# Attention of differences: three row blocks' scores move into the values' projection, and the order of the row blocks changes

## The chip, the cores and the metric

The kernel runs on one core of a Trainium2 chip. The metric is the time of one execution on the device, in microseconds (us), and the figure compared is the median of several executions.

## What is computed

Four layers in a row on a sequence of 1024 rows and 1024 features, in f32. The first two (a dilated attention and a latent attention) and the large MLPs are untouched. The change lies in the mixer of the third and of the fourth layer, which are alike. In them the core of the reference is:

```python
proj = h @ w_in[l]
q_da, k_da, v_da, q_r, k_r, v_r, g_r, u_pool = jnp.split(proj, split_points, axis=-1)
...
lam = (jnp.exp(jnp.sum(lq1.astype(jnp.float32) * lk1.astype(jnp.float32)))
       - jnp.exp(jnp.sum(lq2.astype(jnp.float32) * lk2.astype(jnp.float32))) + lam_init)
...
    s = jnp.einsum('bhmqd,bhmkd->bhmqk', q_blk, k).astype(jnp.float32) * scale
...
```

Each of four heads has two maps (m) of 64 features. Both maps get a causal softmax over the keys, and the output of the head is (softmax of map 0 minus lam times softmax of map 1) times the values of 128 features, normalised per row. Beside it the mixer has a retention of four heads, and a mean over windows of 2, 4, 8 and 16 rows ("pool"). The three outputs are joined and projected by w_out.

## The kernel before

Every engine has its own program, and the order of work is written out by hand in each: the PE program issues matmuls in the order of the code, and waits stand where an instruction needs another engine's result. All matmuls are recorded by one helper, so that a row of the profile says L130 and is told apart by its tiles.

**Projection.** `pe_mix` makes the parts of `h @ w_in` in the order `PARTS = [3, 0, 1, 4, 5, 2]`; part 2, the last, is the values v_da (tile c_v). `pe_tiles` makes a part of eight row tiles in two groups of four (g or b is 0 and 1), each over eight weight blocks k. A weight block is loaded by SP into one of eleven slots (`NS = 11`, tile wst), and split by POOL into whi and wlo; a product takes three matmuls (thi*whi, thi*wlo, tlo*whi). The four tiles of either group of part 2 lie in PSUM banks 0 to 3 (ring "proj"), and ACT copies them to c_v.

**Attention.** The work is cut into 32 units of one head h and one block j of 128 query rows; a unit of block j sees j + 1 blocks of keys, so its width w is 128 * (j + 1). `UNITS` gives the order: in each head j goes 7, 6, ... 0. The PE loop of `pe_diff` does in its iteration i:

- the scores of unit i: for both maps, a matmul of c_q with c_k per 512 keys (64 rows of the array, ps<-c_k,c_q), then a small bf16 matmul that adds the causal mask (ps<-cst_cmask,cst_idb). Map 0 has banks 0 and 1, map 1 banks 2 and 3 (ring "s2"), whatever the width, and the scores of a unit wait until ACT has read those of the unit before,
- a turn of the window output (`WINDOWS`, ps<-s_wa,r_pw) or of the retention's (`RET_TURNS`, ps<-cst_ident,c_rn) in some iterations,
- the transposes of unit i-3's probabilities (ps<-cst_ident,tfl or r_p) into banks 4 and 5,
- the product of unit i-4's transposed probabilities with the values (ps<-c_v,tfl or tfi) into bank 6 or 7.

DVE does per iteration: the maxima of both maps (TENSOR_REDUCE cst_sm<-ps), the low half of a window or retention output (tlo<-ps,thi), which needs ACT's high half, then the mixing of the two maps of unit i-1 (SCALAR_TENSOR_TENSOR tfl<-p_p,cst_sm,tfl), then the copy of the second half of unit i-3's transposes. ACT does: the two exponentials of unit i (tfl, r_p or p_p<-ps,cst_sm), a high half (thi<-ps), the copy of the first four transposed blocks of unit i-3, and the scaling and the squares of unit i-4's output. So the chain through a unit is: scores, maximum of map 0, exponential of map 0, scores of the next unit.

Of the kernel before, what the change touches and what calls it, by code (L numbers as in the profile page):

```python
# [16 lines left out]
NS = 11  # L17
# [156 lines left out]
class Banks:  # L174
# [4 lines left out]
             "s3": [(0,), (1,)], "t3": [(2,), (3,)], "d3": [(4,), (5,)], "o3": [(6,)], "a3": [(7,)], "t2": [(4,), (5,)], "o2": [(6,), (7,)],  # L179
# [94 lines left out]
class Kernel:  # L274
# [355 lines left out]
    def pe_tiles(self, pe, st, nk, items, nb, ring, terms, wkey, ready, kready=None, after=None, amid=None):  # L630
# [4 lines left out]
        for g, size in enumerate(sizes):  # L635
# [3 lines left out]
            for it in group:  # L639
                B.take((st, it), ring)  # L640
# [1534 lines left out]
    def pe_mix(self, q, l):  # L2175
# [8 lines left out]
        for n in self.PARTS:  # L2184
            def amid(b, k):
# [11 lines left out]
            self.pe_tiles(q, ("c", l, n), 8, items, (3, 3, 2) if n == 3 and l == 0 else 4, "proj", terms, lambda k: ("c", l, n, k),  # L2197
# [7 lines left out]
    def act_mix(self, q, l):  # L2205
# [151 lines left out]
    def sp_borrow(self, sp, l):  # L2357
# [39 lines left out]
    def pe_diff(self, q, l):  # L2397
        S, B, ps = self.S, self.B, self.ps
        q.wait_ge(*S.at("mask"))
        for i in range(32 + 4):  # L2400
            if i < 32:
                h, j = self.UNITS[i]
                w = 128 * (j + 1)
                bs = [B.take(("cs", l, i, mp), "s2") for mp in range(2)]
                q.wait_ge(*B.done(("ct", l, "q", 7)))
                q.wait_ge(*B.done(("ct", l, "k", 7)))
                for c in range(0, w, 512):
                    n = min(512, w - c)
                    for mp in range(2):
                        if c == 0:  # L2410
                            for event in B.freed(("cs", l, i, mp)):
                                q.wait_ge(*event)
                        r = slice(64 * mp, 64 * mp + 64)
                        q.matmul(ps[:, bs[mp] + c // 512, 0:n], self.cq[r, h, blk(j)], self.ck[r, h, c:c + n], start=True,
                                 stop=(c + n < w), skip_group_check=True)
                for mp in range(2):
                    q.matmul(ps[:, bs[mp] + c // 512, n - 128:n], self.idb[:], self.cmask[:], start=False, stop=True,
                             skip_group_check=True).then_inc(*S.up("qk", ("c", l, i, mp)))
            if i in self.WINDOWS and self.WINDOWS[i][1] is not None:
# [34 lines left out]
    def act_diff(self, q, l):  # L2454
        S, B, ps = self.S, self.B, self.ps
        for i in range(32 + 4):
            if i < 32:
                h, j = self.UNITS[i]
                w = 128 * (j + 1)
                for mp in range(2):  # L2460
                    key = ("cs", l, i, mp)
                    b = B.of(key)
                    q.wait_ge(*S.at("c_max", (l, i, mp)))
                    if mp == 0:
                        if i >= 4:
                            q.wait_ge(*S.at("turned", ("cT", l, i - 4, self.UNITS[i - 4][1] // 4)))
                    elif i >= 2:
                        q.wait_ge(*S.at("c_mix", (l, i - 2)))
                    dst = self.p1[i % 4] if mp == 0 else self.p2[i % 2]
                    q.activation(dst[:, 0:w], ps[:, b:b + 2, :].rearrange("p a b -> p (a b)")[:, 0:w], ACT.Exp,  # L2470
                                 bias=self.cstat(i, 2 + mp), accum_out=self.cstat(i, 4 + mp)).then_inc(*B.free(key, "exp"))
            if i in self.WINDOWS and self.WINDOWS[i][1] is not None:
# [39 lines left out]

    def act_diff_hi(self, q, l, h):
# [7 lines left out]
    def dve_diff(self, q, l):  # L2521
        S, B, ps = self.S, self.B, self.ps
        q.wait_ge(*S.at("tile", (("c", l, 2), 7)))
        q.memset(self.pw[:], 0.0).then_inc(*S.up("pw_zero", l))
        q.memset(self.wa[:, 0:16], 0.0)
        q.memset(self.wb[:, 0:16], 0.0).then_inc(*S.up("mix_zero", l))
# [791 lines left out]
```

## Time and profile before

| | us |
|---|---|
| median of 3 runs | 4079.43 (4076.68 to 4085.45) |
| the profiled execution, its own time | 4081.01 |
| its span in the trace | 4079.2 |
| PE busy | 3882.3 |
| DVE busy | 2207.4 |
| ACT busy | 1436.9 |
| POOL busy | 1906.9 |
| attention of the third layer, scores of unit 0 to the first matmul of the output projection | 1899.46 to 2060.22 |
| the same of the fourth layer | 3113.24 to 3275.48 |

The two attention stages are 160.8 and 162.2 us of the span. A busy PE is not a PE at its peak: the matmuls' ends are modelled, and at the lower clock the same matmul is counted longer. The granted clock (PEclk) is 1.00 for 2.4 GHz and 0.50 for 1.2 GHz.

### The profile page before, as it was taken

Reading aid. Unit: us, or ns where it says so; the run is one execution under the profiler, and the core shown is the slowest. Engines: PE = TensorE matmul, PEld = TensorE weight load, DVE = VectorE, ACT = ScalarE, POOL = GpSimd, SP = SyncE. Lnnn points to the kernel's source line nnn. Section 1 sums busy time; section 2 is a strip of 40 time slices with the busy share of each in tenths; the row PEclk is TensorE's granted clock in tenths of the full one; section 3 lists DMA queues with packets and bytes.
Section 4 is the critical chain, followed back from the end, with each engine's and each line's share of the span. In section 5 each row is a group of like instructions: output and inputs, shape, how many; then the busy total and the mean of one; then the engine's idle time right before and its main releaser. Section 6 shows DMA issues by size and latency. Waiting matters only on the chain.

```text
span 4079.2 us, 49896 instructions
## 1 busy us (share of the span) xinstructions
PE 3882.3 (95%) x19191; PEld 3140.4 (77%) x19191; DVE 2207.4 (54%) x3488; ACT 1436.9 (35%) x2928; POOL 1906.9 (47%) x1707
## 2 busy tenths in 40 slices
PE   8999999999999999999898999999998898999998
PEld 4677788777888887786576788888786577788887
DVE  2242426482777775632637777624633638777633
ACT  1122223133666662222634333312222634333211
POOL 1313122272333334522234788986522135778975
PEclk9999999999999999999899999999998899999999
DMA  5312221232000003110022222453210033222543
GB/s 178 115 51 79 67 64 42 86 103 62 6 10 7 11 6 110 64 33 17 1 97 96 83 80 86 149 170 123 96 36 8 1 107 97 77 88 78 172 158 129
DMA packets 247508, 310.37 MB, mean 76 GB/s; under 512 B 38804, under 2 KB 161060, under 8 KB 247272
## 3 DMA queue, kind: packets, MB, share of 16 engines
q1 hardware_dynamic: 214456, 231.87, 18.5%
q10 hardware_dynamic: 32816, 75.32, 5.3%
q8 instruction: 152, 2.49, 0.2%
q14 instruction: 84, 0.69, 0.1%
HBM read 253.48 MB, written 51.53 MB: 75 GB/s over the span
## 4 chain that ended last, share of the span: by engine, by line
PE 73%; DVE 16%; ACT 4%; issue 4%; POOL 2%; DMA 1%; ACTq 0%; SPq 0%; DVEq 0%; POOLq 0%
PE ps L130 69%; PE ps L133 4%; DVE cst_sm L153 3%; DVE ml_p L142 3%; ACT thi L136 2%; DVE da_sg L159 1%; POOL wlo L142 1%; DVE tlo L142 1%; DVE f_ta L150 1%; DVE f_tb L150 1%; ACT ml_o L136 1%; ACT tfi L136 0%; POOL whi L139 0%; DVE tfl L142 0%; POOL mlo_z L142 0%
## 5 line engine op out<-in xcount | busy, mean ns | idle before, releaser
L139 POOL CAST whi<-wst 128x512 fp32r<-128x512 f32 (+3 forms) x524 | 424.5, 810 | 1429.8 <-DMA wst<-in_a_w_in 457.7
L142 POOL TENSOR_TENSOR wlo<-wst,whi 128x512 fp32r<-128x512 f32 (+2 forms) x650 | 926.8, 1433 | 42.1
L130 PE MATMUL ps<-whi,thi 128*128 128x512 f32 (+3 forms) x1816 | 707.5, 390 | 19.8 <-POOL wlo L142 6.0
L130 PE MATMUL ps<-whi,tlo 128*128 128x512 f32 (+3 forms) x1816 | 685.2, 377 | 0.0
L130 PE MATMUL ps<-wlo,thi 128*128 128x512 f32 (+3 forms) x1816 | 684.2, 377 | 0.0
L130 PEld LDWEIGHTS ps<-whi,thi 128*128 128x128 f32 x1816 | 344.5, 190 | 102.6 <-issue 25.6
L130 PEld LDWEIGHTS ps<-wlo,thi 128*128 128x128 f32 x1816 | 344.7, 190 | 58.1 <-issue 3.8
L130 PEld LDWEIGHTS ps<-whi,tlo 128*128 128x128 f32 x1816 | 343.7, 189 | 57.5
L130 PE MATMUL ps<-thi,whi 128*128 128x512 f32 x856 | 339.4, 397 | 15.7 <-POOL wlo L142 10.9
L130 PE MATMUL ps<-tlo,whi 128*128 128x512 f32 x856 | 337.8, 395 | 0.0
L130 PE MATMUL ps<-thi,wlo 128*128 128x512 f32 x856 | 337.3, 394 | 0.0
L153 DVE TENSOR_REDUCE cst_sm<-ps 128x1 f32<-128x1024 f32 (+7 forms) x256 | 246.5, 984 | 75.5 <-PE ps L130 75.5
L130 PEld LDWEIGHTS ps<-thi,whi 128*128 128x128 f32 x856 | 163.4, 191 | 53.1 <-POOL wlo L142 13.6
L130 PE MATMUL ps<-mla_kh,thi 128*128 128x512 f32 x512 | 192.0, 416 | 1.9 <-ACT tfi L136 1.9
L150 DVE SCALAR_TENSOR_TENSOR f_tb<-f_ub,tfi,f_tb 128x1024 f32<-128x1024 f32 x88 | 190.7, 2167 | 1.6
L130 PEld LDWEIGHTS ps<-thi,wlo 128*128 128x128 f32 x856 | 163.5, 191 | 34.7
L130 PEld LDWEIGHTS ps<-tlo,whi 128*128 128x128 f32 x856 | 163.5, 191 | 33.8
L136 ACT ACTIVATE thi<-ps 128x512 fp32r<-128x512 f32 (+2 forms) x258 | 141.1, 565 | 137.4 <-PE ps L133 132.8
L136 ACT ACTIVATE whi<-wst 128x512 fp32r<-128x512 f32 x126 | 70.5, 620 | 279.1 <-DVE wst L142 241.3
L130 PE MATMUL ps<-c_k,c_q 64*128 64x512 f32 (+3 forms) x384 | 131.8, 631 | 36.4 <-ACT tfl L136 35.1
L142 POOL TENSOR_TENSOR tlo<-tfl,thi 128x512 fp32r<-128x512 f32 x96 | 152.8, 1597 | 6.1 <-ACT thi L136 1.1
L145 POOL TENSOR_SCALAR tfl<-tfl,cst_sm 128x64 f32<-128x64 f32 x128 | 56.7, 443 | 182.5 <-DVE cst_sm L159 176.2
(389 smaller groups left out, 8244.6 us busy)
## 6 DMA issues: line engine op xcount, KB each, us to landing
wst<-in_w_down SPq DMA_DIRECT2D x140, 256.0 KB, 3.2
wst<-in_w_up SPq DMA_DIRECT2D x126, 256.0 KB, 3.0
scr_h<-f_tb SPq DMA_DIRECT2D x44, 512.0 KB, 4.0
wst<-in_w_in SPq DMA_DIRECT2D x64, 256.0 KB, 2.7
wst<-in_a_w_in SPq DMA_DIRECT2D x72, 192.0 KB, 2.4
wst<-in_ada_w SPq DMA_DIRECT2D x48, 256.0 KB, 3.4
da_am<-in_ada_w SPq DMA_DIRECT2D x48, 256.0 KB, 2.7
f_T2lw<-scr_h SPq DMA_DIRECT2D x48, 256.0 KB, 3.8
```

Source lines behind the costliest of these rows:

```text
L130: return self.none if self.e is None else self.e.matmul(*a, **k)
L133: return self.none if self.e is None else self.e.transpose(*a)
L136: return self.none if self.e is None else self.e.activation(*a, **k)
L139: return self.none if self.e is None else self.e.tensor_copy(*a)
L142: return self.none if self.e is None else self.e.tensor_tensor(*a)
L145: return self.none if self.e is None else self.e.tensor_scalar(*a)
L150: return self.e.scalar_tensor_tensor(out=out, in0=a, scalar=s, in1=b, op0=o1, op1=o2, **k)
L153: return self.none if self.e is None else self.e.tensor_reduce(*a, **k)
L159: return self.none if self.e is None else self.e.reciprocal(*a)
```

## The change

- Units 0, 1 and 2 are scored inside the second group of part 2, before its weight blocks k = 2, 4 and 6 (`FIRST_UNITS`). The second group's four tiles take banks 4 to 7 (ring "tr4"), so that banks 0 to 3 are there for the scores. ACT does the three units' exponentials before it copies the second group's tiles, and DVE's loop starts with them; its clearing of r_pw, s_wa and s_wb stands behind unit 3's maxima.
- The order of a head is j = 7, 5, 0, 4, 6, 3, 1, 2.
- A unit with j below 4 needs one bank for each map and takes it from the ring "s1", banks 0, 2, 1, 3 in turn.
- The window outputs are turned at iterations 8, 9, 15 and 16 instead of 5, 6, 11 and 12.
- The weights of part 2 start in slot 9, so that the planes and slots which units 0 to 2 write are free by then. In the third layer six slots are passed over (3 to 8); in the fourth the part began in slot 9 already. SP's instructions stay the same in number and order.

```diff
@@ class Banks @@
-             "s3": [(0,), (1,)], "t3": [(2,), (3,)], "d3": [(4,), (5,)], "o3": [(6,)], "a3": [(7,)], "t2": [(4,), (5,)], "o2": [(6,), (7,)],
+             "s1": [(0,), (2,), (1,), (3,)], "s3": [(0,), (1,)], "t3": [(2,), (3,)], "d3": [(4,), (5,)], "o3": [(6,)], "a3": [(7,)], "t2": [(4,), (5,)], "o2": [(6,), (7,)],
@@ def pe_tiles @@
-                B.take((st, it), ring)
+                B.take((st, it), ring if isinstance(ring, str) else ring[g])
@@ def sp_mix @@
+            while n == 2 and self.wn % NS != 9:
+                self.wn += 1
@@ def pe_mix, amid(b, k) @@
+                if n == 2 and b and k in self.FIRST_UNITS:
+                    self.pe_scores(q, l, self.FIRST_UNITS[k])
...
+                          ("proj", "tr4") if n == 2 else "proj", terms, lambda k: ("c", l, n, k),
@@ def act_mix @@
+                if n == 2 and b:
+                    for i in range(3):
+                        self.act_exp(q, l, i)
@@ units @@
-    UNITS = [(h, j) for h in range(4) for j in range(7, -1, -1)]
+    UNITS = [(h, j) for h in range(4) for j in (7, 5, 0, 4, 6, 3, 1, 2)]
-    WINDOWS = {1: (0, None), 5: (0, 0), 6: (0, 1), 7: (1, None), 11: (1, 0), 12: (1, 1)}
+    WINDOWS = {8: (0, 0), 9: (0, 1), 15: (1, 0), 16: (1, 1)}
+    FIRST_UNITS = {2: 0, 4: 1, 6: 2}
@@ def pe_diff, act_diff @@
-        for i in range(32 + 4):
+        for i in range(3, 32 + 4):
@@ def pe_scores @@
+        bs = [B.take(("cs", l, i, mp), "s1" if j < 4 else "s2") for mp in range(2)]
@@ def act_exp @@
+            if mp == 0:
+                if i >= 4:
+                    q.wait_ge(*S.at("turned", ("cT", l, i - 4, self.UNITS[i - 4][1] // 4)))
+                else:
+                    q.wait_ge(*S.at("tile", ("w", ("c", l, 2, i))))
+            elif i >= 2:
+                q.wait_ge(*S.at("c_mix", (l, i - 2)))
```

On PE, at the end of the values' projection of the third layer (matmuls with whi, wlo, thi and tlo are the projection) and the start of the attention, the program before reads:

```order
 L130 MATMUL ps<-wlo,thi 128x512
 L130 MATMUL ps<-whi,tlo 128x512
 L130 MATMUL ps<-c_k,c_q 128x512 x4
 L130 MATMUL ps<-cst_cmask,cst_idb 128x128 x2
 L130 MATMUL ps<-c_k,c_q 128x512 x2
 L130 MATMUL ps<-c_k,c_q 128x384 x2
 L130 MATMUL ps<-cst_cmask,cst_idb 128x128 x2
 L130 MATMUL ps<-c_k,c_q 128x512 x2
```

and the program of the change reads, in the middle of the projection, at unit 1:

```order
 L130 MATMUL ps<-wlo,thi 128x512
 L130 MATMUL ps<-whi,tlo 128x512
 L130 MATMUL ps<-c_k,c_q 128x512 x2
 L130 MATMUL ps<-c_k,c_q 128x256 x2
 L130 MATMUL ps<-cst_cmask,cst_idb 128x128 x2
 L130 MATMUL ps<-whi,thi 128x512
 L130 MATMUL ps<-wlo,thi 128x512
 L130 MATMUL ps<-whi,tlo 128x512
```

Before, nothing but a wait stands between the scores of the first three units; now 24 matmuls of the projection do, and at its end the first transposes (of unit 0) follow the scores of unit 3.

On PE in the second head, from the scores of unit 10 on (c_k,c_q are scores, cst_ident transposes, c_v the product with the values), the program of before is:

```order
 L130 MATMUL ps<-c_k,c_q 128x384 x2
 L130 MATMUL ps<-cst_cmask,cst_idb 128x128 x2
 L133 MATMUL ps<-cst_ident,tfl 128x128 x6
 L130 MATMUL ps<-c_v,tfi 128x128 x7
 L130 MATMUL ps<-c_k,c_q 128x256 x2
 L130 MATMUL ps<-cst_cmask,cst_idb 128x128 x2
 L133 MATMUL ps<-cst_ident,r_p_167 128x128 x5
 L130 MATMUL ps<-c_v,tfl 128x128 x6
```

and that of the change:

```order
 L130 MATMUL ps<-c_k,c_q 128x128 x2
 L130 MATMUL ps<-cst_cmask,cst_idb 128x128 x2
 L133 MATMUL ps<-cst_ident,r_p_167 128x128 x3
 L130 MATMUL ps<-c_v,tfl 128x128 x2
 L130 MATMUL ps<-c_k,c_q 128x512 x2
 L130 MATMUL ps<-c_k,c_q 128x128 x2
 L130 MATMUL ps<-cst_cmask,cst_idb 128x128 x2
 L133 MATMUL ps<-cst_ident,tfl 128x128 x8
```

The first of the two pieces is from units 13 and 14 of before (j = 2 and 1), the second from units 10 and 11 of the change (j = 0 and 4): long runs of transposes and value products stood behind narrow scores, and now narrow scores have few of them behind them and a wide unit has eight transposes.

## Rows read from the trace of the kernel before

**Rows 1.** The page: the chain that ended last, by engine.
```profile
PE 73%; DVE 16%; ACT 4%; issue 4%; POOL 2%; DMA 1%; ACTq 0%; SPq 0%; DVEq 0%; POOLq 0%
```
**Rows 2.** Stretches of both layers: length, busy time and instructions, granted clock.
```profile
core 0: us, PE busy (x) PEld busy (x) DVE busy (x) ACT busy (x) POOL busy (x), PEclk, DMA share, GB/s
1855.68:1899.46 43.78, 43.69 (x193) 35.89 (x192) 3.13 (x9) 6.57 (x12) 0.00 (x0) 1.00 0.00 1
1899.46:1917.99 18.53, 11.85 (x31) 5.11 (x31) 9.31 (x15) 7.30 (x13) 9.20 (x6) 0.65 0.06 12
1917.99:2051.42 133.43, 116.66 (x635) 77.90 (x635) 91.68 (x167) 79.55 (x234) 26.68 (x24) 0.86 0.00 1
2051.42:2060.22 8.80, 7.61 (x66) 6.91 (x65) 3.78 (x14) 7.66 (x30) 1.98 (x3) 1.00 0.42 130
...
3113.24:3131.30 18.06, 11.38 (x30) 4.56 (x30) 9.79 (x15) 7.29 (x13) 9.19 (x6) 0.69 0.06 12
3131.30:3266.39 135.09, 117.06 (x635) 77.75 (x635) 92.22 (x167) 79.59 (x234) 26.66 (x24) 0.85 0.00 1
3266.39:3275.48 9.09, 7.87 (x65) 6.92 (x65) 3.78 (x14) 7.95 (x30) 2.53 (x4) 1.00 0.46 129
```
**Rows 3.** Waits within 1899 to 2060: total us, times, longest.
```profile
ACT tfl L136 <- DVE cst_sm L153: 48.1, 24, 4.8
...
DVE cst_sm L153 <- PE ps L130: 35.4, 21, 4.9
```
**Rows 4.** Timeline of PE, third head: start, us, instruction, count, idle before.
```profile
1978.27 1.99 PE L130 MATMUL ps<-c_k,c_q 64*128 64x512 f32 x8
...
1982.97 2.90 PE L130 MATMUL ps<-c_k,c_q 64*128 64x512 f32 x8 [1.27 <-ACT tfl L136]
...
1988.35 2.96 PE L130 MATMUL ps<-c_k,c_q 64*128 64x512 f32 x8 [1.37 <-ACT tfl L136]
...
2002.35 1.95 PE L130 MATMUL ps<-c_v,tfl 128*128 128x128 f32 x16
2004.23 0.92 PE L130 MATMUL ps<-c_k,c_q 64*128 64x384 f32 x4
...
2011.69 0.49 PE L130 MATMUL ps<-c_k,c_q 64*128 64x128 f32 x4
...
2014.13 0.99 PE L130 MATMUL ps<-c_k,c_q 64*128 64x512 f32 x2
```
**Rows 5.** Timelines of DVE and ACT, the softmax of a unit with j = 7.
```profile
1980.46 2.36 DVE L153 TENSOR_REDUCE cst_sm<-ps 128x1 f32<-128x1024 f32 x2 [2.36 <-PE ps L130]
...
1981.71 1.11 ACT L136 ACTIVATE tfl<-ps,cst_sm 128x1024 f32<-128x1024 f32 x1 [2.54 <-DVE cst_sm L153]
...
1983.86 0.19 ACT L136 ACTIVATION_READ_ACCUMULATOR p_p<-ps,cst_sm 128x1 f32 x1
```
**Rows 6.** Timeline of DVE, unit 21, an iteration with a retention output.
```profile
2006.04 1.01 DVE L153 TENSOR_REDUCE cst_sm<-ps 128x1 f32<-128x384 f32 x2
2008.17 0.42 DVE L142 TENSOR_TENSOR tlo<-ps,thi 128x256 fp32r<-128x256 f32 x1 [1.11 <-ACT thi L136]
...
2009.96 0.74 DVE L153 TENSOR_REDUCE cst_sm<-ps 128x1 f32<-128x256 f32 x2
```
**Rows 7.** Timeline of PE, units 25 and 26, at a clock of 0.50 from 2023.
```profile
2019.13 3.72 PE L130 MATMUL ps<-c_k,c_q 64*128 64x512 f32 x8 [1.27 <-ACT tfl L136]
...
2025.38 3.92 PE L130 MATMUL ps<-c_k,c_q 64*128 64x512 f32 x8 [0.50 <-ACT tfl L136]
...
2031.60 1.22 PE L130 MATMUL ps<-c_k,c_q 64*128 64x512 f32 x1 [0.90 <-ACT tfl L136]
```
**Rows 8.** Timelines of DVE and POOL: mixing 384 keys twice, and POOL's windows.
```profile
1938.12 2.33 DVE L150 SCALAR_TENSOR_TENSOR tfl<-p_p,cst_sm,tfl 128x384 f32<-128x384 f32 x1
...
2052.25 0.62 DVE L150 SCALAR_TENSOR_TENSOR tfl<-p_p,cst_sm,tfl 128x384 f32<-128x384 f32 x1
...
1938.14 1.89 POOL L142 TENSOR_TENSOR s_wa<-s_wb 128x1024 f32<-128x1024 f32 x1
```
**Rows 9.** The page's loads of w_in, and POOL's split of a weight block.
```profile
wst<-in_w_in SPq DMA_DIRECT2D x64, 256.0 KB, 2.7
...
1850.43 0.61 POOL L139 CAST whi<-wst 128x512 fp32r<-128x512 f32 x1 [0.84 <-DMA wst<-in_w_in]
1851.12 1.29 POOL L142 TENSOR_TENSOR wlo<-wst,whi 128x512 fp32r<-128x512 f32 x1
```

More of the change, by code:

```diff
@@ L2398, in pe_diff @@
         S, B, ps = self.S, self.B, self.ps
-        q.wait_ge(*S.at("mask"))
-        for i in range(32 + 4):
+        for i in range(3, 32 + 4):
             if i < 32:
[L2402 to L2419, printed above, removed]
+                self.pe_scores(q, l, i)
+            if i in self.WINDOWS:
                 self.pe_window(q, l, *self.WINDOWS[i])
@@ L2444, in pe_diff, with pe_scores @@
             self.pe_diff_turn(q, l, h, "tr4")
+    FIRST_UNITS = {2: 0, 4: 1, 6: 2}
+    def pe_scores(self, q, l, i):
+        S, B, ps = self.S, self.B, self.ps
+        q.wait_ge(*S.at("mask"))
+        h, j = self.UNITS[i]
+        w = 128 * (j + 1)
+        bs = [B.take(("cs", l, i, mp), "s1" if j < 4 else "s2") for mp in range(2)]
+        q.wait_ge(*B.done(("ct", l, "q", 7)))
+        q.wait_ge(*B.done(("ct", l, "k", 7)))
+        for c in range(0, w, 512):
+            n = min(512, w - c)
+            for mp in range(2):
+                if c == 0:
+                    for event in B.freed(("cs", l, i, mp)):
+                        q.wait_ge(*event)
+                r = slice(64 * mp, 64 * mp + 64)
+                q.matmul(ps[:, bs[mp] + c // 512, 0:n], self.cq[r, h, blk(j)], self.ck[r, h, c:c + n], start=True,
+                         stop=(c + n < w), skip_group_check=True)
+        for mp in range(2):
+            q.matmul(ps[:, bs[mp] + c // 512, n - 128:n], self.idb[:], self.cmask[:], start=False, stop=True,
+                     skip_group_check=True).then_inc(*S.up("qk", ("c", l, i, mp)))
     def pe_diff_turn(self, q, l, h, ring):
@@ L2449, in pe_diff_turn, with banks @@
                          [self.S.at("c_scaled", (l, h))])
+    def banks(self, b, w):
+        return self.ps[:, b, 0:w] if w <= 512 else self.ps[:, b:b + 2, :].rearrange("p a b -> p (a b)")[:, 0:w]
     def cstat(self, i, n, w=1):
@@ L2455, in act_diff @@
         S, B, ps = self.S, self.B, self.ps
-        for i in range(32 + 4):
+        for i in range(3, 32 + 4):
             if i < 32:
[L2458 to L2472, printed above, removed]
+                self.act_exp(q, l, i)
+            if i in self.WINDOWS:
                 m, hf = self.WINDOWS[i]
@@ L2511, in act_diff, with act_exp @@
             self.act_diff_hi(q, l, h)
+    def act_exp(self, q, l, i):
+        S, B, ps = self.S, self.B, self.ps
+        w = 128 * (self.UNITS[i][1] + 1)
+        for mp in range(2):
+            key = ("cs", l, i, mp)
+            b = B.of(key)
+            q.wait_ge(*S.at("c_max", (l, i, mp)))
+            if mp == 0:
[5 more added lines that the diff above has]
+                q.wait_ge(*S.at("c_mix", (l, i - 2)))
+            dst = self.p1[i % 4] if mp == 0 else self.p2[i % 2]
+            q.activation(dst[:, 0:w], self.banks(b, w), ACT.Exp,
+                         bias=self.cstat(i, 2 + mp), accum_out=self.cstat(i, 4 + mp)).then_inc(*B.free(key, "exp"))
     def act_diff_hi(self, q, l, h):
@@ L2522, in dve_diff @@
         S, B, ps = self.S, self.B, self.ps
[L2523 to L2526, printed above, removed]
         for i in range(32 + 4):
@@ L2534, in dve_diff @@
                     q.wait_ge(*S.at("qk", ("c", l, i, mp)))
-                    q.tensor_reduce(self.cstat(i, 2 + mp), ps[:, b:b + 2, :].rearrange("p a b -> p (a b)")[:, 0:w], AXX,
+                    q.tensor_reduce(self.cstat(i, 2 + mp), self.banks(b, w), AXX,
                                     ALU.max, negate=True).then_inc(*S.up("c_max", (l, i, mp)))
-            if i == 2:
+            if i == 3:
+                q.wait_ge(*S.at("tile", (("c", l, 2), 7)))
+                q.memset(self.pw[:], 0.0).then_inc(*S.up("pw_zero", l))
+                q.memset(self.wa[:, 0:16], 0.0)
+                q.memset(self.wb[:, 0:16], 0.0).then_inc(*S.up("mix_zero", l))
+            if i == 7:
                 q.wait_ge(*S.at("ld_mix", l))
@@ L2540, in dve_diff @@
                     *S.up("v_seq", ("sgm", l)))
-            if i in self.WINDOWS and self.WINDOWS[i][1] is not None:
+            if i in self.WINDOWS:
                 m, hf = self.WINDOWS[i]
```

4 lines of the change are left out of this document (2 added, 2 removed).

## The prediction

> **What bounds the kernel now.** The page's chain [rows 1] says that PE carries 73% of what ended last, DVE 16%. That is an average over all stages, so the next view is the two stages that the change touches, cut at their joints [rows 2]. In the values' projection (1855.68 to 1899.46) PE is busy all the time at clock 1.00 while DVE works 3.1 and ACT 6.6 of 43.8 us: PE alone bounds it. From 1899.46 to 1917.99, units 0 to 2, PE is busy only 11.9 of 18.5 us, and that at clock 0.65: nothing but three softmaxes one after another, since scores wait for the exponentials of the unit before. The fourth layer has the same, 18.06. From unit 3 to unit 31's scores it takes 133.4 and 135.1 us, with DVE busy 92 and ACT 80: no engine is full. The waits [rows 3] say how it turns: ACT waits 48 us for DVE's maxima, DVE 35 us for PE's scores, and PE in turn waits for ACT at the wide units, 1.27 and 1.37 us in [rows 4]. A loop of latencies bounds the wide units, PE's own work the narrow ones.
>
> **Part 1: three units inside the projection.** Removed: 18.5 and 18.1 us before unit 3's scores, mean 18.3. Added to the projection: PE's work for the three units. With its banks free a unit of j = 7 takes from 1978.27 to the maxima at 1980.46 [rows 4, 5], 2.2 us; one of j = 0 takes 0.5 and the mask's 0.2 [rows 4], 0.7; j = 5 lies between, 1.8. Sum 4.7. The step from projection to scores shows a start at 1899.46 where the matmul before it began at 1898.98 and the usual spacing is 43.78 / 192 = 0.23, so some 0.25 is lost at such a step; there are six, of which I count 1.0 in all. Part 1 costs 5.7 and gives 12.6 per layer. The bounds of the six steps are 0 and 6 x 0.5 = 3.0.
> The Trainium skill (TensorEngine Tiling (Array Packing), Key Properties) says that a change of the tiling mode drains the engine, which speaks against 64-row matmuls between 128-row ones. By that rule with 0.5 a step the part would give 10.6 instead of 12.6.
> Its cover: after unit 0's scores PE has two weight blocks, 2 x 43.78 / 16 = 5.5 us, before unit 1's. The softmax of unit 0 takes from the maxima at 1980.46 to the last exponential at 1984.05 [rows 5], 3.6 us, and unit 1's first scores need only map 0's. Margin 1.9 us. If that cover were gone, PE would stop for up to 3.6 us a unit in the projection. ACT copies the first group before that, and the second group's tiles behind unit 2's exponentials, which fall before the group's end; unit 0's transposes wait for that copy, some 1 us behind unit 3's scores, which hide it.
> Moved: in the third layer the weights of part 2 skip six slots. Its first block then waits until PE is through with block 3 of part 5 (eight blocks at 2.74 us that end at 1855.68), four blocks before that end, at 1844.7; it lands 2.7 later and is split in 1.9 [rows 9], at 1849.3, and PE wants it at 1855.7. Margin 6.4 us, the same for the following blocks, which come as fast as PE uses them. Cost nothing; with the cover gone it would be the excess over 6.4, once.
>
> **Part 2: the order.** I lay out one head at full clock, scores to scores, without window or retention outputs. Pieces: wide unit to wide unit 4.70 and 5.38 [rows 4], growing about 0.4 with each key block (maximum and exponential 0.14 each, scores 0.2); eight blocks of value product 1.95, so 0.24 a block [rows 4]; a transpose 0.12.
> Old order, 7 to 0: 4.7, 5.4, 4.8, 4.5 by the loop, then by PE (scores + transposes + product of wide units) 4.3, 3.6, 3.0, 2.5. Sum 32.8.
> New order: 7 to 5 4.7; 5 to 0 4.9; 0 to 4 2.9 (scores of map 1 wait for the second exponential of 5, and DVE mixes unit 7 first); 4 to 6 3.5; 6 to 3 5.5 by PE (2.9 + 6 transposes + 8 blocks); 3 to 1 3.3; 1 to 2 1.9 (own banks, no wait); 2 to 7 3.5 by PE. Sum 30.2.
> Retention outputs: there DVE's loop is maximum, both exponentials, ACT's high half, DVE's low half, mixing, copy; for unit 21 it is 3.92 us [rows 6]. Before, these eight iterations hold j = 3 to 0 and cost 1.2 a head over the plain ones. Now they hold 6, 3, 1, 2; by the same pieces unit 20 takes 5.5, and the delays add up to 3.9 at the next head. Windows: four iterations, 4.2 before, 3.9 now. Whole, from unit 3 to unit 31: before 19.9 + 35.0 + 34.0 + 31.3 = 120.2, now 17.8 + 33.4 + 34.8 + 29.0 = 115.0. The order gives 5.2. The traced 133.4 and 135.1 stand 13 to 15 above my sum, and I keep that rest but for two changes.
> First, the clock: at 0.86 over 133.4 us, 2 x 0.14 x 133.4 = 37 us ran at half. The cycle 25 to 26 takes 6.25 at half [rows 7] and its equal 17 to 18 5.38 [rows 4]: 16%, so 37 us hold 5.1 us of loss. The low stretches stand where wide units follow each other; now at most two do. I take half of it back, 2.6; bounds 0 and 5.1.
> Second, POOL: DVE's mixing of 384 keys takes 2.33 us beside POOL's windows and 0.62 without [rows 8]. Before, the first windows ran at units 0 and 1 with DVE idle; now they run at units 3 to 5, and three mixings meet them. DVE has 1 to 2 us of slack there; I charge 1.5, bounds 0 and 3 x 1.7 = 5.1.
> The Trainium skill (SBUF — State Buffer, Who interferes with whom) says that a VectorE instruction with two SBUF inputs contends with a GpSimd instruction that reads SBUF. By that rule the trace agrees, and the case in which it decides is the second rival below.
>
> **Part 3: the end.** From unit 31's scores to the output projection it takes 8.8 and 9.1 us [rows 2]. What is still to be transposed and multiplied then were units of j = 3, 2, 1, 0 (10 blocks; with the product of j = 4 15) and are now 6, 3, 1, 2 (16 and 21): six more of each, 6 x 0.36 = 2.2, and a longer last mixing. Loss 2.5. Weights of w_out are asked for at the same retention turn (unit 31) as before and have that much longer.
>
> Per layer: 12.6 + 5.2 + 2.6 - 1.5 - 2.5 = 16.4; two layers 32.8. From the execution of the trace, 4081.0, that is 4048.2; it stands 1.6 above the median shown, so the forecast for the median is **4047**.
>
> **Rivals.** (a) *The clock stays up.* If waits of PE are all short, the whole 5.1 comes back and half of what is left of the rest, (14 - 5.1) / 2 = 4.4, goes too: 16.4 + 2.5 + 4.4 = 23.3 per layer, 4033. For it: PE's work per head (36 blocks at 0.24 and 0.12, scores 0.5 + 0.21 a block, in all 24.6) fills 30.2 us better than 32.8. Against: PE's waits are 1.3 us at a time already in [rows 4], and the clock is 0.86 all the same.
> (b) *The order gives nothing.* Retention outputs beside a wide unit, and mixings beside POOL's, eat the 5.2, and no clock comes back: 12.6 - 1.5 - 2.5 = 8.6 per layer, 4062; with the upper bound on POOL 5.0, 4069. For it: DVE is then busy 92 of 128 us, in a loop that also holds ACT. Against: half of these iterations are narrow.
> (c) *The projection waits.* If unit 0's softmax is not done at block 4, PE stops there: 1.9 us margin, at most 3.6 for each of two units, so 9 per layer left, 4061. Speaks against it that DVE and ACT are idle there.
> (d) *Slower.* If the scores inside it brought the projection's second half down to clock 0.50, its 21.9 us would take as much again: 16.4 - 21.9 = -5.5 per layer, 4090. It decides from 16.4 us of PE time lost there on. In [rows 2] the clock is 1.00 wherever PE has no gaps and 0.65 where it waits a third of the time; the scores bring no wait of that size.
> (e) *Nothing moves*: softmax in the projection hidden but given back at the end, since the end waits for weights. They are asked for at unit 31 in any case, so hardly possible.
>
> **How the numbers follow.** Forecast (4040 to 4055) 0.45; (a) 0.23; (b) 0.20; (c) 0.06; (d) 0.04; (e) 0.02. The range goes from (a) with a little more to (b)'s worse bound: 4028 to 4067. A measurement tells 0.2%, 8 us, from no change. Faster by more than that, below 4071: all but (d) and (e), 0.94; same 0.03; slower 0.03.
>
> **What would show it.** Right: c_k,c_q matmuls three times inside the second half of the values' projection with PE idle before none of them for ACT, that half about 5.7 us longer at clock 1.00; unit 3's scores right behind it; 33 to 36 us from one unit of j = 7 to the next; a clock above 0.86; mixings of 1.5 to 2.5 us beside s_wa at units 3 to 5; 11 us from unit 31's scores to the output projection. Wrong: an idle PE in front of unit 1's or 2's scores, maxima that start long after their scores in iterations 8, 9, 16, 20 and 28, or a head above 36 us. The estimate stands weakest on the rest of 14 us that I carry over.

## The result and the profile after

The changed kernel takes 4046.63 us (median of 4 runs, 4041.24 to 4050.95) where the kernel before, in the same series, took 4078.05 (4075.16 to 4085.45): a ratio of 0.992, with a 95% interval of 0.9908 to 0.9932. The forecast was 4047. This section and the one on why the forecast was right show that the sum came out right while several of its terms did not.

The page of the changed kernel names the same engines in its chain as [rows 1]:

```profile
PE 72%; DVE 16%; ACT 4%; issue 4%; POOL 2%; DMA 1%; ACTq 0%; SPq 0%; DVEq 0%; POOLq 0%
```

The stages, cut as in [rows 2] (the first six rows are the third layer: the values' projection up to unit 3's scores, units 3 to 8, 8 to 16, 16 to 24, 24 to 31, and the end up to the output projection; the last three are the fourth layer's projection, units 3 to 31, and end):

```profile
core 0: us, PE busy (x) PEld busy (x) DVE busy (x) ACT busy (x) POOL busy (x), PEclk, DMA share, GB/s
1857.59:1905.97 48.38, 48.38 (x220) 37.53 (x218) 15.63 (x21) 12.79 (x24) 10.38 (x10) 1.00 0.07 23
1905.97:1925.44 19.47, 16.46 (x107) 10.90 (x107) 16.21 (x33) 11.86 (x36) 9.79 (x6) 1.00 0.08 12
1925.44:1962.03 36.59, 31.81 (x180) 21.68 (x179) 27.91 (x43) 21.85 (x67) 26.94 (x23) 0.91 0.00 0
1962.03:1997.58 35.55, 30.70 (x184) 21.48 (x183) 24.17 (x49) 23.01 (x71) 0.94 (x2) 0.95 0.01 1
1997.58:2031.86 34.28, 27.97 (x157) 19.85 (x156) 23.18 (x44) 21.68 (x60) 0.00 (x0) 0.87 0.00 1
2031.86:2044.30 12.44, 10.63 (x84) 9.12 (x83) 5.19 (x16) 9.69 (x34) 4.06 (x5) 0.95 0.38 113
3055.57:3103.94 48.37, 48.37 (x219) 37.53 (x217) 10.68 (x21) 12.78 (x24) 0.00 (x0) 1.00 0.00 1
3103.94:3230.22 126.28, 105.46 (x621) 72.97 (x620) 91.58 (x166) 78.33 (x228) 37.57 (x30) 0.93 0.01 3
3230.22:3244.53 14.31, 11.95 (x83) 10.40 (x83) 6.17 (x18) 10.30 (x34) 4.42 (x6) 0.88 0.43 134
```

PE is busy through the whole projection at clock 1.00, which is now 48.4 us instead of 43.8 in [rows 2]: 4.60 for three units, and nothing in front of unit 3. Units 3 to 31 take 125.9 and 126.3 us (before 133.4 and 135.1), the end 12.4 and 14.3 (before 8.8 and 9.1). From the start of the third layer's values' projection to its output projection it is 186.7 us, before 204.5 (1855.68 to 2060.22): 17.8 less. In the fourth it is 189.0 against 206.0, which is 17.0 less. The forecast had 16.4 each. The two stages give 34.9; the spans differ by 31.9. Over all the traces here, what lies between the stages differs by up to 2.4 us, what lies behind them by 3.0, and what lies ahead of them by 6.6 (the values' projection starts at 1852.1 to 1858.7).

The scores in the projection, on PE's timeline (start, us, instruction, count, idle before), with the projection's own matmuls left out:

```profile
1884.88 1.99 PE L130 MATMUL ps<-c_k,c_q 64*128 64x512 f32 x8
1886.80 0.28 PE L130 MATMUL ps<-cst_cmask,cst_idb 128*128 128x128 bf16 x2
...
1892.55 1.56 PE L130 MATMUL ps<-c_k,c_q 64*128 64x512 f32 x8
...
1899.80 0.49 PE L130 MATMUL ps<-c_k,c_q 64*128 64x128 f32 x4
1900.22 0.28 PE L130 MATMUL ps<-cst_cmask,cst_idb 128*128 128x128 bf16 x2
...
1905.97 1.24 PE L130 MATMUL ps<-c_k,c_q 64*128 64x512 f32 x6
```

No row has an idle time. The three units take 2.20, 1.78 and 0.71 us from first to last matmul, 4.69, and the projection grew by 4.60: beyond the scores' own extent the six steps between projection and scores cost nothing. Counted from start to start, as the forecast did, a step takes 0.32 us (the matmul before unit 0's scores starts at 1884.56, the scores at 1884.88) where the projection's spacing is 0.23: some 0.1 a step, which is then part of the 4.60. ACT is done with unit 0 at 1890.66:

```profile
1888.33 1.12 ACT L136 ACTIVATE tfl<-ps,cst_sm 128x1024 f32<-128x1024 f32 x1 [4.73 <-DVE cst_sm L153]
...
1890.47 0.19 ACT L136 ACTIVATION_READ_ACCUMULATOR p_p<-ps,cst_sm 128x1 f32 x1
```

That is 1.9 us before unit 1's scores at 1892.55, the margin of the forecast.

### The profile page after: what moved, and what is told of

Its sections match the earlier page's. It is cut to its first block, busy times and chain, and to the rows that moved or that the text cites. A ratio compares the mean times of both kernels' runs of the same rounds, so it can differ in the third digit from the quotient of the medians.

```text
span 4047.3 us, 49898 instructions
## 1 busy us (share of the span) xinstructions
PE 3858.2 (95%) x19191; PEld 3133.4 (77%) x19191; DVE 2216.1 (55%) x3488; ACT 1436.6 (35%) x2928; POOL 1912.2 (47%) x1707
## 4 chain that ended last, share of the span: by engine, by line
PE 72%; DVE 16%; ACT 4%; issue 4%; POOL 2%; DMA 1%; ACTq 0%; SPq 0%; DVEq 0%; POOLq 0%
PE ps L130 68%; PE ps L133 4%; DVE cst_sm L153 3%; DVE ml_p L142 3%; ACT thi L136 2%; DVE da_sg L159 1%; DVE tlo L142 1%; POOL wlo L142 1%; DVE f_ta L150 1%; DVE f_tb L150 1%; ACT ml_o L136 1%; ACT tfi L136 1%; POOL mix_z L142 0%; DVE tfl L142 0%; POOL whi L139 0%
## 5 line engine op out<-in xcount | busy, mean ns | idle before, releaser
L130 PE MATMUL ps<-whi,thi 128*128 128x512 f32 (+3 forms) x1816 | 709.2, 391 | 19.5 <-POOL wlo L142 7.4
L130 PE MATMUL ps<-thi,whi 128*128 128x512 f32 x856 | 339.6, 397 | 15.3 <-POOL wlo L142 11.7
L136 ACT ACTIVATE tfi<-ps,cst_sm 128x1024 f32<-128x1024 f32 (+1 forms) x160 | 130.7, 817 | 24.8 <-DVE cst_sm L153 20.1
## 6 DMA issues: line engine op xcount, KB each, us to landing
wst<-in_a_w_in SPq DMA_DIRECT2D x72, 192.0 KB, 2.5
```

The source lines that it names most:

```text
L130: return self.none if self.e is None else self.e.matmul(*a, **k)
L136: return self.none if self.e is None else self.e.activation(*a, **k)
```

## The experiments

All times are medians. The stage time is from the start of the values' projection to the output projection in the profiled execution, third and fourth layer.

| kernel | us | stages, us |
|---|---|---|
| before | 4078 to 4080 | 204.5, 206.0 |
| the change | 4046.63, again 4044.08 | 186.7, 189.0; again 188.5, 187.6 |
| placement alone (with the new window places) | 4040.63 | 186.7, 187.5 |
| order, ring and window places alone | 4063.40 | 197.2, 197.4 |
| window places alone | 4063.48 | 197.8, 198.2 |
| narrow units on two banks a map | 4045.94 | 188.2, 188.8 |
| no window sums, in the change | 4031.16 | 182.0, 182.0 |
| no window sums, before | 4071.04 | 203.3, 201.8 |
| new order in heads 1 and 2 only | 4036.32 | 184.7, 184.6 |
| the same, windows later | 4044.45 | 187.6, 186.5 |
| placement alone, windows later | 4055.69 | 194.7, 192.8 |
| unit 0 a block later | 4048.00 | 188.5, 192.0 |
| window sums in halves | 4040.59 | 185.2, 187.5 |

### The parts of the change

**Placement alone.** The order is put back, all units are on "s2".

```diff
-    UNITS = [(h, j) for h in range(4) for j in (7, 5, 0, 4, 6, 3, 1, 2)]
+    UNITS = [(h, j) for h in range(4) for j in range(7, -1, -1)]
-        bs = [B.take(("cs", l, i, mp), "s1" if j < 4 else "s2") for mp in range(2)]
+        bs = [B.take(("cs", l, i, mp), "s2") for mp in range(2)]
```

> The change with the order of the row blocks put back to 7, 6, ... 0 and all units on two banks a map; units 0 to 2 stay in the projection, the windows at iterations 8, 9, 15, 16. My theory (the placement carries most): the three units removed 18.3 us and the projection grew by 4.6 in the trace of the change, so 13.7 per layer, less up to 1.5 for POOL's windows beside the mixings, and the end stays at 9: 24 to 27 us in all, 4051 to 4054. Rival 1 (the order carries half): 4060 or more. Rival 2 (the order gives nothing in sum, its longer end eats it): 4047, as the change.

4040.63 us, ratio to before 0.9911 (0.9896 to 0.9925). What the second rival says of the order is true, it gives nothing in sum, and the placement (here with the new window places) is worth more than any of the cases had. Its stages (third layer, the six cuts as above):

```profile
1854.65:1904.33 49.68, 49.68 (x224) 37.91 (x222) 17.36 (x21) 14.08 (x24) 10.36 (x10) 1.00 0.07 22
1904.33:1922.00 17.67, 15.50 (x119) 11.72 (x118) 14.83 (x33) 11.25 (x36) 10.65 (x6) 1.00 0.07 14
1922.00:1959.90 37.90, 31.99 (x180) 20.58 (x180) 28.67 (x45) 23.12 (x68) 27.96 (x24) 0.91 0.00 0
1959.90:1995.75 35.85, 32.68 (x184) 21.75 (x183) 23.61 (x49) 21.80 (x66) 0.08 (x1) 0.86 0.01 1
1995.75:2032.54 36.79, 31.19 (x161) 20.65 (x160) 23.77 (x44) 23.25 (x66) 0.00 (x0) 0.86 0.00 1
2032.54:2041.32 8.78, 7.61 (x66) 6.90 (x65) 3.77 (x14) 7.63 (x29) 1.96 (x3) 1.00 0.42 123
```

Against these the new order gains 1.3 us in the projection (its three units are narrower), loses 1.8 in units 3 to 8, gains 1.3, 0.3 and 2.5 in the three heads behind, and loses 3.7 at the end: together 0.05 us worse, and in the fourth layer 1.4. The change run again gives 1.8 and 0.1 us worse.

**Order alone.** Units 0 to 2 go back behind the projection (`FIRST_UNITS = {}`, the loops of PE and ACT from 0, no exponentials in `act_mix`).

> The change with units 0 to 2 taken out of the projection again; order, rings and window places of the change. Theory: unit 3 to unit 31 gains 7.5 and 8.8 us by the trace of the change, the end loses 3.6 and 5.2, so 3.8 per layer; in front the units 7, 5, 0 need some 2 us less than 7, 6, 5. Together 8 to 12 us: 4066 to 4070. Rival (order and placement only help together): within 3 us of before, 4075 to 4078. Rival (the order carries more than the placement): below 4060.

4063.40 us, 0.996 (0.9947 to 0.9973). Better than I expected, and placement (39 us below before) plus this (16) is far more than both together (31 to 35): the two kernels share a part. They share the new places of the windows; they also share the second group's banks 4 to 7, DVE's later clearing and the weights' slots, so the next run takes the windows' places by themselves.

**Window places alone.** One line of the kernel before:

```diff
-    WINDOWS = {1: (0, None), 5: (0, 0), 6: (0, 1), 7: (1, None), 11: (1, 0), 12: (1, 1)}
+    WINDOWS = {8: (0, 0), 9: (0, 1), 15: (1, 0), 16: (1, 1)}
```

> The kernel before with one edit: the window outputs are turned at iterations 8, 9, 15, 16 instead of 5, 6, 11, 12. The question is why units 3 to 8 took 23.4 us before and 17.7 with the placement alone. Theory A (the windows' places): the two turns leave iterations 5 and 6 and POOL's second set of sums no longer starts at iteration 7, where DVE's operations took 1.44 to 2.33 us instead of 0.22 to 0.62; 3 to 4 us less there, 1 us more in the second head: 2 to 3 per layer, 4072 to 4075. Theory B (the granted clock at the entry, 0.50 before and 1.00 behind the projection, explains all 5.7): 4077 to 4080 here.

4063.48 us, 0.9965 (0.9952 to 0.9977): theory A, but more than twice its size. The stages of this kernel (units 3 to 8, 8 to 16, 16 to 24, 24 to 31), and under them the same of before:

```profile
1919.12:1937.40 18.28, 17.81 (x116) 13.23 (x116) 13.26 (x31) 11.56 (x36) 0.00 (x0) 0.88 0.01 1
1937.40:1975.32 37.92, 31.99 (x179) 20.81 (x178) 28.66 (x44) 23.19 (x68) 27.97 (x24) 0.91 0.00 0
1975.32:2009.75 34.43, 30.68 (x184) 20.33 (x183) 23.63 (x49) 21.86 (x66) 0.07 (x1) 0.95 0.01 1
2009.75:2045.85 36.10, 30.21 (x159) 20.34 (x158) 23.77 (x44) 23.31 (x66) 0.00 (x0) 0.86 0.00 1
```

```profile
1917.99:1941.40 23.41, 19.82 (x121) 13.93 (x121) 17.05 (x32) 11.97 (x36) 6.96 (x4) 0.91 0.00 1
1941.40:1978.27 36.87, 32.00 (x177) 20.44 (x177) 28.78 (x48) 22.96 (x69) 19.72 (x21) 0.91 0.00 0
1978.27:2014.14 35.87, 31.77 (x182) 21.48 (x181) 22.08 (x44) 21.34 (x66) 0.00 (x0) 0.86 0.01 1
2014.14:2051.42 37.28, 33.06 (x160) 22.06 (x159) 23.77 (x44) 23.27 (x66) 0.00 (x0) 0.77 0.00 1
```

Units 3 to 8 take 18.3 instead of 23.4 us, the second head 1.0 more, the last two 1.4 and 1.2 less at a higher clock. Together 6.7 us in the third layer and 7.8 in the fourth. Of the 5.1 in the first stretch, 0.9 each is from the turns out of iterations 5 and 6 (cycles 4.20 and 3.65, now 3.29 and 2.75), and 3.3 from the cycle of unit 7 to 8 (5.52, now 2.20). There DVE stood beside POOL's second sums; the timeline of DVE in the kernel before:

```profile
1936.64 1.44 DVE L150 SCALAR_TENSOR_TENSOR cst_sm<-cst_sm,cst_lam 128x1 f32<-128x1 f32 x1
...
1941.15 1.52 DVE L150 SCALAR_TENSOR_TENSOR cst_sm<-cst_sm,cst_lam 128x1 f32<-128x1 f32 x1
```

An operation on one column, 0.22 us elsewhere, takes 1.4 to 1.5, twice around one narrow unit, with the 2.33 of [rows 8] between them. How much of the 3.3 is the sums' can be read from a run further down, the kernel before without the sums: there this cycle takes 3.08 us, so 2.4 are the sums' and 0.9 are not. On PE it is one wait, in the kernel before and, under it, without the sums:

```profile
1940.70 0.49 PE L130 MATMUL ps<-c_v,tfi 128*128 128x128 f32 x2 [2.79 <-DVE tfi L139]
```

```profile
1935.02 0.49 PE L130 MATMUL ps<-c_v,tfi 128*128 128x128 f32 x2 [0.34 <-DVE tfi L139]
```

So the three parts, each as the difference of two kernels, in the third and the fourth layer: window places 6.7 and 7.8 (before to window places), placement 11.2 and 10.6 (window places to placement alone; the second group's banks and the slots move with it), order with ring 0.0 and -1.4 (placement alone to the change).

**The ring.** `"s1" if j < 4 else "s2"` becomes `"s2"`.

> The change with the one-bank ring taken out: narrow units take two banks a map again, so the scores of j = 3, 1 and 2 wait for the exponentials of the unit before. My sum had 1.9 us from j = 1 to j = 2 with banks of their own where about 3 us would be needed without. Theory: 1 to 2 us a head, 8 to 14 us in all: 4055 to 4061. Rival (PE's transposes and products stand between them anyway, the banks are free in time): within 2 us of the change, 4045 to 4049.

4045.94 us, 0.9922 (0.9907 to 0.9937): the theory falls. The cycle of j = 1 to 2 does grow (1.63 to 2.83 us in the second head), but the one behind it shrinks (4.61 to 4.31), and units 24 to 31 take 34.9 instead of 34.3. In the stages it is 1.3 us in all, too little for the medians to tell.

**The heads apart.**

```diff
+    UNITS = [(h, j) for h in range(4) for j in ((7, 5, 0, 4, 6, 3, 1, 2) if h in (1, 2) else range(7, -1, -1))]
```

> The change with the new order in the second and third head alone; the first and the last head go 7, 6, ... 0. Theory (what the order gives is set head by head, by the stretches of the two traces): against the placement alone the new order gave 1.3 us in the second head and 0.3 to 1.5 in the third; in the last it gave 2.5 and cost 3.7 to 5.2 at the end, in the first it cost 0.5. So this kernel is 1.6 to 2.8 per layer better than the placement alone, 5 us better than the change or more: 4035 to 4038. Rival (the heads can't be taken apart, since the clock makes up the difference): 4040 to 4046.

4036.32 us, 0.9897 (0.9884 to 0.9911), the lowest median of a kernel that keeps the whole computation. Its interval overlaps that of the placement alone, so the medians don't part the two; the stages, 184.7 and 184.6 us, are 2.0 and 3.0 below the placement alone, and the end is back at 9.5 and 9.1. In these traces the new order pays in the middle heads, where its wide last units don't stand at the stage's end.

**The cover.** Unit 0 is scored before k = 3, so that one weight block is left between units 0 and 1.

```diff
-    FIRST_UNITS = {2: 0, 4: 1, 6: 2}
+    FIRST_UNITS = {3: 0, 4: 1, 6: 2}
```

> The change with unit 0 scored one weight block later, before k = 3, so that only one block (2.74 us) lies between units 0 and 1. I had counted a softmax of 3.6 us that the cover must hide. Theory: PE waits 0.8 to 0.9 us in front of unit 1 in each layer, nothing else moves: 1.7 us, 4048 with the change at 4046.6, and the waiting place is seen in the trace. Rival (the wait also lowers the granted clock in the projection): 5 us a layer and more, 4056. Rival (map 0's bank is free after 2.4 us already, so no wait): 4046.6.

4048.00 us, 0.9923 (0.991 to 0.9937). The projection is 49.24 us instead of 48.38 in both layers: 0.86, as the theory has it. (The fourth layer's 192.0 in the table holds a cycle of 7.9 us from unit 7 to 8; the change without this edit has it at 4.6 and 7.7 in one trace and at 6.2 and 4.8 in the other.) PE and ACT at that place:

```profile
1891.37 2.44 PE L130 MATMUL ps<-c_k,c_q 64*128 64x512 f32 x8
```

```profile
1890.99 1.11 ACT L136 ACTIVATE p_p<-ps,cst_sm 128x1024 f32<-128x1024 f32 x1
1892.00 0.19 ACT L136 ACTIVATION_READ_ACCUMULATOR p_p<-ps,cst_sm 128x1 f32 x1
```

The wait is not in front of unit 1 but inside it: map 0's scores find their banks free, map 1's wait for the exponential that ends at 1892.1, so that the eight matmuls take 2.44 us instead of 1.56. A timeline row that gathers matmuls can hide such a wait in its length.

### POOL's sums and DVE

**Without the sums.** In `pool_windows` one subtraction is left of each window; once in the change, once in the kernel before.

```diff
-            op(q.tensor_tensor(wa[:, 16:1040], u[:, 16:1040], u[:, 15:1039], ALU.add))
...
-            q.tensor_tensor(pl, pl, u[:, 16:1040], ALU.subtract).then_inc(*S.up("windows", (l, m)))
+            q.tensor_tensor(pl, u[:, 16:1040], u[:, 15:1039], ALU.subtract).then_inc(*S.up("windows", (l, m)))
```

> The change with POOL's sums over windows left out: one subtraction is left of each of the two windows' 6 to 8 operations, so the pool output is not the reference's. Theory: the clash of POOL's windows with DVE's mixings costs the 1.5 us per layer that I charged, up to 3 where unit 10's maxima were late: 3 to 6 us in all, 4041 to 4044. Rival (it lies in DVE's slack): 4046 to 4047.5.

> The kernel before with POOL's sums over windows left out (one subtraction is left of each), so the pool output is not the reference's. In the change the same edit gave 15.5 us. Theory (the change brought a new clash, since the first sums ran beside idle DVE before): here only the second sums cost, 3 to 4 us a layer: 4071 to 4073. Rival (the clash cost as much before, my charge of 1.5 for the difference holds): 12 to 15 us, 4063 to 4066.

4031.16 us in the change (0.9886, 0.9869 to 0.9902) and 4071.04 in the kernel before (0.9978, 0.9969 to 0.9987). In the stages the change loses 4.7 and 7.0 us with the sums gone, the kernel before 1.2 and 4.3: the sums cost the change 3.1 us per layer more on average. By the medians they cost 15.5 us in the change (12.9 against its second series) and 9.4 in the kernel before, so 1.7 to 3.0 more per layer. The stages hold 11.7 of the 15.5; for the rest the traces name no cause. DVE's busy time between units 3 and 31 falls from 91.5 to 83.4 us in the change:

```profile
1903.05:2022.65 119.60, 102.77 (x622) 71.65 (x621) 83.39 (x166) 78.00 (x228) 16.79 (x18) 0.94 0.02 3
```

Where it strikes in the change, fourth layer, DVE and POOL, and PE behind them:

```profile
3116.76 3.34 DVE L150 SCALAR_TENSOR_TENSOR tfl<-p_p,cst_sm,tfl 128x896 f32<-128x896 f32 x1
3120.02 0.74 DVE L153 TENSOR_REDUCE cst_sm<-ps 128x1 f32<-128x256 f32 x2
```

```profile
3116.79 2.36 POOL L142 TENSOR_TENSOR s_wa<-s_wa,c_pu 128x1024 f32<-128x1024 f32 x1
```

```profile
3118.78 0.28 PE L130 MATMUL ps<-cst_cmask,cst_idb 128*128 128x128 bf16 x2
3122.03 1.75 PE L133 MATMUL ps<-cst_ident,tfl 128*128 128x128 f32 x7 [2.97 <-ACT tfi L136]
```

A mixing of 896 keys takes 3.34 us instead of 1.15, the maxima of unit 6 start after it, 3.1 us behind their scores, and the cycle from unit 7 to 8 is 7.7 us, where it is 3.7 without the sums.

**Windows later.** To find what decides the price, the windows were turned at 11, 12, 18, 19, once with the mixed heads and once with the placement alone. The change ran again beside them.

> The changed kernel itself, in one series with the two below, so that they stand beside it and not beside a figure of another series. Expected 4045 to 4048; its two stages 186.7 and 189.0 us from the start of the values' projection to the output projection, with the fourth layer's cycle from unit 7 to 8 either 4.6 or 7.7.

> The kernel with the new order in the second and third head alone, and the window outputs at iterations 11, 12, 18, 19 instead of 8, 9, 15, 16. So POOL's second sums, which started behind iteration 9 and stood beside units 10 and 11 (cycle 6.5 instead of 5.3), start behind iteration 12. Theory (a sum costs where it stands beside a wide mixing): 1 to 2 us less at units 10 and 11, and up to as much again at the wide unit 16: 0 to 4 us in all, 4033 to 4036. Rival (it costs the same anywhere): 4036 to 4037, and rival (the two outputs of iterations 18 and 19 push the retention's): 4039 or more.

> The placement alone, order 7, 6, ... 0, with the window outputs at iterations 11, 12, 18, 19. Here the second sums stood beside units 10 and 11 (cycle 7.7 instead of 5.3) and would stand beside j = 3 to 0 and unit 16. Theory: the cycle from 10 to 11 comes back to 4.8 to 5.3, 2.4 less a layer, the turns in narrow iterations cost 0.9 each as they did at 5 and 6, and 1 us more at unit 16: 0 to 3 us in all, 4038 to 4041. Rival: the turns and sums beside narrow units stop PE as in the kernel before (7 to 8 took 5.5 instead of 2.2): 4045 or more.

4044.08 us (0.9912, 0.9896 to 0.9927), 4044.45 (0.9918, 0.9904 to 0.9931) and 4055.69 (0.9943, 0.9929 to 0.9957). Both late kernels are slower than their partners, by 8 and 15 us (by 4.9 and 13.3 in the two stages), so my theory that a sum costs where it stands beside a wide mixing falls. In the kernel with the placement alone the cycle of unit 13 to 14 (1953.34 to 1961.29) went from 3.3 to 8.0 us. DVE and POOL there and in the two cycles behind it:

```profile
1954.82 2.44 DVE L150 SCALAR_TENSOR_TENSOR r_p<-p_p,cst_sm,r_p 128x640 f32<-128x640 f32 x1
...
1963.05 2.39 DVE L150 SCALAR_TENSOR_TENSOR cst_sm<-cst_sm,cst_lam 128x1 f32<-128x1 f32 x1
```

```profile
1954.69 1.89 POOL L142 TENSOR_TENSOR s_wa<-s_wb 128x1024 f32<-128x1024 f32 x1
1956.66 2.81 POOL L142 TENSOR_TENSOR s_wb<-s_wa 64x1024 f32<-64x1024 f32 x1
...
1963.07 2.35 POOL L142 TENSOR_TENSOR s_wa<-s_wa,c_pu 128x1024 f32<-128x1024 f32 x1
```

The operation on one column begins at 1963.05 and ends at 1965.44; POOL's begins at 1963.07 and ends at 1965.42. The mixing of 640 keys ends at 1957.26, 0.68 after POOL's first operation at 1956.58 (alone it takes 0.89), and POOL's next lasts 2.81 us instead of 1.89, with the rest of that mixing in its first 0.6. In these rows DVE waits until POOL's operation is through, and what it pays is the rest of that operation, not a share of its own width. The Trainium skill (SBUF — State Buffer, SBUF: two separate sides) says that the two engines' shared pair of ports is an "exclusive lock", held for the whole instruction and not a split of the bandwidth; these rows agree, and I had read only the clash out of the skill, not the lock. The page gives the pair to whichever starts first; here DVE's operation is recorded 0.02 us ahead of POOL's and waits all the same, so the rows don't settle that part.

What the unit pays is a second thing. PE in the cycle from 13 to 14, and under it the same products in the placement alone:

```profile
1957.79 0.69 PE L133 MATMUL ps<-cst_ident,tfl 128*128 128x128 f32 x2 [2.87 <-DVE tfi L139]
1958.27 3.09 PE L130 MATMUL ps<-c_v,tfi 128*128 128x128 f32 x14
```

```profile
1952.39 1.73 PE L130 MATMUL ps<-c_v,tfi 128*128 128x128 f32 x14
```

PE waits 2.87 us for DVE's copy, which stands behind the long mixing, and the 14 products after the wait take 1.36 us more, in a stretch whose granted clock is 0.79. The 2.39 us of the one-column operation fall into the next cycle, which takes 2.74 us as in the placement alone; the one behind it takes 3.44 instead of 3.11. A narrow unit has two two-input operations of DVE in 2.2 to 3.3 us, a wide one two in 5, which speaks for the sums being worst beside narrow units; but the edit moves the turns too, the third head is also 3.3 and 1.4 us longer, and no run parts the sums' share from the turns'. The expectation's rival of the two turns at 18 and 19 stays open with it.

**Sums in halves.** The same sums, each large operation as two of 512 columns (504 in the scaling):

```diff
-            op(q.tensor_tensor(wa[:, 16:1040], u[:, 16:1040], u[:, 15:1039], ALU.add))
+            def two(f):
+                f(16, 528)
+                return f(528, 1040)
+            op(two(lambda a, b: q.tensor_tensor(wa[:, a:b], u[:, a:b], u[:, a - 1:b - 1], ALU.add)))
```

> The changed kernel with POOL's large two-input operations of the window sums each cut into two halves of the columns: the same sums, the same result. In the traces a two-input operation of DVE that starts beside such a sum ends when the sum ends (a 128x1 one at 1963.05 took 2.39 us, the sum ran 1963.07 to 1965.42). Theory (DVE waits for the rest of POOL's running operation): half as long an operation is half the wait; without the sums the two stages were 11.7 us shorter, so 4 to 7 us come back, 4037 to 4040 against 4044 to 4047 of the change. Rival (the two engines share by bytes, so the number of operations means nothing): 4044 to 4047.

4040.59 us, 0.991 (0.9896 to 0.9923). The stages are 3.0 us shorter in all than the change's (3.4 against its second trace), less than the 4 to 7 expected. In each layer's 32 units the small operations took 10.5 and 10.2 us in the change and 8.8 and 10.2 here, the mixings 31.7 and 33.1 and now 32.5 and 32.1. The change's second trace has 11.0 and 11.3, 31.8 and 30.9, so the mixings did not get shorter: single waits of the small operations did, and there are more of them. The direction fits the lock; the size, 3 us, is at the edge of what the runs tell, and it was not shown that a finer cut would give more.

## Why the forecast was right, point by point

**Part 1.** Right in kind, a little low. Predicted 12.6 us per layer. In the change the stretch up to unit 3's scores fell from 62.3 to 48.4 us in the third layer and from 61.8 to 48.4 in the fourth, 13.7 on average. Its terms: removed 18.3, as [rows 2]; scores and steps together 5.7, measured 4.60. With the old order (window places alone to placement alone) the stretch fell from 62.3 to 49.7 us. That this is 12.6 too is chance, since the units there are wider; and of it 11.2 and 10.6 were left at the output projection, because units 16 to 31 then ran 2.1 us longer (third layer), in the third head at clock 0.86 instead of 0.95. The Trainium skill (TensorEngine Tiling (Array Packing), Key Properties) has a change of the tiling mode drain the engine; these runs don't show whether it does, but the price of 0.5 a step that I had tried for it, and its 10.6 us, are refuted. The margin was 1.9 us as forecast, and with the cover halved the projection grew by 0.86. The skipped slots cost nothing: PE has no wait in the projection, and the layer that skips six has the same 48.4 us as the one that skips none. The end of the projection hides unit 2's softmax and the copies.

**Part 2.** Wrong in its terms, right in its sum by their cancelling, which was luck. The windows were entered as 4.2 before and 3.9 after, 0.3 of gain; their new places are worth 6.7 and 7.8 us. Two things failed there. I had given a turn nearly the same price beside every unit. With the window places alone moved, the cycles of iterations 8, 9 and 16 take 4.71, 5.37 and 4.71 us, as the bare 4.70, 5.38 and 4.70 do [rows 4]; only the turn at 15 costs 0.9 (3.11 instead of 2.20), as those at 5 and 6 did. And I had not asked what POOL starts behind a turn: the second sums wait for the second window's turn, and with the turn at iteration 6 they fell on the narrow units 7 and on, 2.4 us in the cycle from 7 to 8. The row for that stood in the forecast [rows 8], at 1938.12, and I took it as a price per mixing, not as the delay of a unit. The sums are not the whole of the gain: the kernel before gains only 1.2 and 4.3 us in its stages when the sums are left out. Why the last two heads also got 1.4 and 1.2 us shorter, at a higher clock, no run shows.

The plain order was entered as 5.2 with the windows, so 4.9 without. Against the placement alone, with the end left out, the new order gave 3.6 us in the third layer (128.2 + 49.7 against 125.9 + 48.4) and 3.8 in the fourth, of which 1.3 is the projection's: the heads gave 2.3 and 2.5. In units 3 to 8 it lost 1.8 and 4.0, since those are now j = 4, 6, 3, 1, 2, with 21 key blocks in place of 15, and the sums strike them (19.5 and 21.7 us, without the sums 17.5). From unit 8 on the sum was close: with the windows' terms left out it had 2.6, -0.1 and 2.3 us for the three stretches, and they gave 1.3, 0.3 and 2.5 in the third layer, 1.3, 1.5 and 3.7 in the fourth. One-bank units gave next to nothing. The rest of 13 to 15 us between the sum and the traced time, which the forecast carried over, is 10.9 and 11.3 in the change, and is still unexplained.

The clock was right as a direction: 0.92 and 0.93 over units 3 to 31, from 0.86 and 0.85 [rows 2], so about half of the low time went. Which part of the change did it can't be given to one edit: the placement puts units 3 to 8 at 1.00 (0.91 before), and the window places alone raise the last two heads from 0.86 and 0.77 to 0.95 and 0.86.

The clash with POOL was entered as 1.5 more, with 5.1 as its bound, and measured 3.1 more per layer by the stages (5.9 in all against 2.7 before), so about twice too small.

**Part 3.** Right in kind, too small: 2.5 predicted, 3.6 and 5.2 measured. I counted six transposes and products more at full clock; the clock at the end is 0.95 and 0.88 now, where it was 1.00. With the last head in the old order the end is 9.5 and 9.1.

**Sum.** Predicted per layer 12.6 + 5.2 + 2.6 - 1.5 - 2.5 = 16.4; measured 17.8 and 17.0. The windows' 7 us, missing from it, stood in for the order's. Rival (b), "the order gives nothing", was true of the order, and its 4062 was wrong for the same missing term. Of the signs that I had named, the good ones came in the main: the scores stand in the projection with PE idle before none, unit 3's right behind it, and the clock is above 0.86. But there was a bad one too: a head of 36.6 us in each layer, above the 36 that I had named. Maxima were on time or less than 0.5 us late at the iterations I had named (8, 9, 16, 20, 28), and 3.8, 2.0 and 3.8 us late at units 10 (behind DVE's mixing of 1024 keys, 2.95 us instead of 1.28), 29 and 30. A right median did not mean that this could be passed over.

## What to carry to other kernels

When an edit moves the place at which an engine waits, look at what the next engine starts behind that place, and lay it over the units that it will then stand beside: here a line that moves four outputs was worth more than half of the main idea. An edit of several parts should be priced and, if it can be, run part by part; here two of three carried it, the third cost what it gave, and keeping it only in the heads where it paid made the kernel with the lowest median here, some 0.2% below the change. Long softmax chains at a stage's start are well hidden in the projection ahead of them, for the price of their matmuls alone, as long as the cover reaches to the last exponential.

## What the runs showed of the hardware that I had not expected

- Two-input operations of DVE and POOL on SBUF don't share: one column took 2.39 us beside a POOL operation of 2.35, and 0.22 alone; POOL's took 2.81 instead of 1.89 behind DVE's. With the sums cut in half the longest of the 32 small operations fell from 1.72 to 0.86 us (third layer) and to 1.02 (fourth).
- Six changes between matmuls of 64 and 128 rows in a busy stretch cost no time beyond the scores' own extent (4.60 us for 4.69 us of scores); from start to start a change takes 0.32 us where the spacing is 0.23.
- Sums that keep POOL busy for 21 us (37.7 less 16.8 between units 3 and 31), while the chain of the whole execution gives POOL 2%, cost 4.7 and 7.0 us of a stage; the rows above show DVE's delays as the way. Sums and turns moved together to other iterations (11, 12, 18, 19) cost the placement alone another 8.0 and 5.2.
